# Rows of four weighted sums two fetches further behind their dots in TensorE's order

## The chip, the cores and the metric

The kernel runs on one core of a Trainium2 chip. The metric is the device time of one execution in microseconds (us): the median of several runs. Besides, one execution was profiled; its own time and its span are given apart, because all durations below come from that one execution. The engines are called by their short names: PE is TensorE (PEld its weight load), DVE is VectorE, ACT is ScalarE, POOL is GpSimd and SP is SyncE, which here only starts DMAs.

## What is computed

One layer of a streaming encoder over 576 tokens in two groups, A (192 tokens) and B (384 tokens). The token-mixing half (projection `w_in`, band attention, short convolution, gates, projection `w_o`) is followed by a retrieval half, and that one takes most of the time. For each token and each of 8 heads it picks the 16 best of 128 x 128 experts, and then gathers the chosen rows of two tables of 16384 x 1024 floats:

```python
idx = jnp.take_along_axis(cand_idx, pos, axis=-1)
g = jax.nn.softmax(top_s, axis=-1).astype(hb.dtype)
u = jnp.take(expert_u, idx, axis=0)
act = jax.nn.gelu(jnp.einsum("thkd,td->thk", u, hb))
vv = jnp.take(expert_v, idx, axis=0)
return jnp.einsum("thk,thkd->td", g * act, vv)
```

So each token has 128 dots with rows of `expert_u`, and its result is the sum of 128 rows of `expert_v` with the weights that come out of those dots.

## The kernel before, in words

**Tiles and fetches.** 32 tokens make a tile g (GT = 32; NG = 18 tiles). A tile has 32 fetches; fetch n = 32 g + j brings, for 128 pairs of a token and an expert, u and v side by side into one slot of the buffer `ring`: 128 x 2048 floats, 1 MB. Each fetch is an indirect DMA that POOL issues (L437), as soon as the fetch that last held the slot has been folded (semaphore `fold`). Up to fetch 192 (EARLY) the fetches have 8 slots, while 3 slots carry weight blocks that SP loads (L449); from there on they have all 11.

**The steps of a fetch.** DVE waits for the row and makes the dots (`dot`, L1492). ACT turns them into a small matrix of weights in three instructions (`spread`, L1081 to L1088, one place later: `gather(n)` on ACT spreads fetch n - 1). PE multiplies the v half by it into PSUM (`fold`, L825), always for four fetches in a row; the four go to four groups of 32 columns of the array. So a fold of four needs all four dots and spreads, and the four slots that it frees are those of the fetches eight further on: the fold of fetches 4K to 4K+3 lets POOL issue 4K+8 to 4K+11.

**After a tile** come `keep_sum` (ACT, L1095), `join` and `residual` (PE, L835 and L844), `scale` and `add` (DVE, L1501 and L1508) and `store`; for the next tile `natural` (PE, L805) and `keep_natural` (ACT, L1065) bring the tokens into rows, and for tiles 0, 4 and 6 `gate_rows` (PE, L813) the gate. They are hung on m, the fetch that is counted from behind n: `join` at j = 4 of the next tile, `residual` at 8, `natural` at 16, `keep_sum` at 31.

**What sets the order.** A list ORDER is written out by hand; each engine walks through it and does its own part of each entry. No engine reorders anything. Its stages, with the spans of the profiled execution:

- 320 to 470 us: retrieval of group A (`rt`; PE L745 and L725, DVE picks L1348 to L1395, `place` L794 on PE and L1478/L1481 on DVE, fetches 0 to 27 in groups of four, one group a head).
- 470 to 1045 us: the rest of group B's work, cut into ticks, stands between the fetches 28 to 171, about one tick a fetch: projection (`z`, L560 and L564), attention (`at`, scores L594, transposes L611, values L627), keys (`kn`, L660), merge (`mg`, L683 and L689), output projection (`wo`, L704), norm (L534) and retrieval (`rt`, L745 and L725).
- from 1075 us on: fetches alone.

PE's `join`, `residual`, `natural`, `gate_rows` and `place` share two PSUM banks. Each waits until the one before it in the order has been read (`g_free`). POOL issues fetches 4h to 4h + 3 of tile 0 only after DVE's `place(0, h)` (semaphore `placed_kept`).

In `merge`, DVE's first instruction for group B (L1317) writes over the buffer that the values leave from, so it waits for three stores `o_v_p` (L456). SP issues those when PE has finished the fourth merge tick and their turn in SP's list comes.

## Time and profile before

| what | value |
| --- | --- |
| median of 3 runs | 2088.72 us (2087.12 to 2089.95) |
| the profiled execution's own time | 2079.57 us |
| its span, first to last instruction | 2077.4 us |
| mean granted clock of TensorE | 0.957 |
| busy share of the span | PE 81%, DVE 59%, ACT 35%, POOL 29% |
| fetches | 576 of 1 MB, 71.3% of the 16 DMA engines' span |

A busy share is a mean over stages with different limits. The table of stretches shows the DMA engines full from about 1080 us to the end, and PE busy without a gap in much of what lies before. In a row of a timeline the brackets at the end give how long the engine had been idle before it and what released it. A matmul on f32 stands as two records; so one fold of four has 16.

### The profile page before, as it was taken

The numbers are of one execution on the slowest core, as the hardware profiler recorded it, in microseconds if no ns is written. First come the engines' busy times: TensorE is split into PE (matmuls) and PEld (weight loads), VectorE is DVE, ScalarE is ACT, GpSimd is POOL, SyncE is SP. The second block draws the span as 40 slices with busy tenths as digits, with TensorE's granted clock in tenths as the row PEclk, the third lists the DMA queues.
The fourth block names the chain that finished last, engine by engine and source line by source line (L and its number), as shares of the span: only waits on it lengthen the run. The fifth ranks groups of instructions, "written<-read, shape, count | busy, mean of one in ns | idle before, by whom it ended". The sixth has DMA issues, their size and how long they took to land.

```text
span 2077.4 us, 22509 instructions
## 1 busy us (share of the span) xinstructions
PE 1690.4 (81%) x7500; PEld 771.4 (37%) x7500; DVE 1221.6 (59%) x3212; ACT 724.9 (35%) x2231; POOL 607.4 (29%) x584
## 2 busy tenths in 40 slices
PE   6999997669978799989967777777777777777776
PEld 3864896435445455445522121121121121121111
DVE  3334116866565454447867777777677675555554
ACT  3125103442475223232343333333333343333332
POOL 0000001332322223222254434434444434333331
PEclk8999999779977999999999999999999999999999
DMA  9546514889965799967799999999999999999995
GB/s 400 212 173 255 221 52 167 341 336 385 358 235 199 315 400 370 421 254 276 269 373 422 421 421 422 421 421 421 421 421 421 422 421 422 421 422 421 421 421 240
DMA packets 102467, 718.50 MB, mean 346 GB/s; under 512 B 13584, under 2 KB 13584, under 8 KB 15696
## 3 DMA queue, kind: packets, MB, share of 16 engines
q0 software_dynamic: 82944, 604.02, 71.3%
q1 hardware_dynamic: 18544, 110.69, 13.6%
q10 hardware_dynamic: 864, 2.36, 0.3%
q8 instruction: 59, 0.97, 0.2%
q14 instruction: 56, 0.46, 0.1%
HBM read 712.30 MB, written 4.73 MB: 345 GB/s over the span
## 4 chain that ended last, share of the span: by engine, by line
DMA 41%; PE 30%; DVE 14%; issue 10%; ACT 4%; POOL 1%; SPq 0%; DVEq 0%; POOLq 0%; ACTq 0%
DMA ring<-in_expert_uv_dram,uidx 40%; PE ps L564 7%; PE ps L825 6%; PE ps L683 5%; DVE ring L1492 5%; PE ps L689 2%; PE ps L704 2%; POOL ring L437 1%; PE ps L560 1%; DMA ring<-in_wpack_dram 1%; PE ps L627 1%; PE ps L594 1%; PE ps L534 1%; ACT wdiag L1088 1%; DVE left L1393 1%
## 5 line engine op out<-in xcount | busy, mean ns | idle before, releaser
L825 PE MATMUL ps<-ring,wdiag 128*32 128x512 f32 x2304 | 866.6, 635 | 246.8 <-ACT wdiag L1088 228.0
L437 POOL DMA_INDIRECT ring<-in_expert_uv_dram,uidx x576 | 606.1, 1052 | 1387.0 <-PE ps L825 959.8
L1492 DVE CUSTOM_DVE_ANT_0 ring<-ring,mA 128x1024 f32<-128x1024 f32 x576 | 700.4, 1223 | 427.8 <-DMA ring<-in_expert_uv_dram,uidx 422.0
L825 PEld LDWEIGHTS ps<-ring,wdiag 128*32 128x32 f32 x2304 | 174.0, 114 | 881.0 <-ACT wdiag L1088 552.4
L1081 ACT ACTIVATE gel<-act_in 128x1 f32<-128x1 f32 x576 | 116.7, 203 | 875.5 <-DVE act_in L1492 875.0
L1088 ACT ACTIVATE wdiag<-repeat,wsel 128x32 f32<-128x32 f32 x576 | 185.1, 321 | 18.8
L1083 ACT ACTIVATE wsel<-gel,gsel 128x1 f32<-128x1 f32 x576 | 169.7, 295 | 18.7
L564 PE MATMUL ps<-hB,ring 128*128 128x384 f32 x320 | 109.3, 493 | 0.0
L745 PE MATMUL ps<-hB,ring 128*128 128x384 f32 x256 | 89.4, 504 | 8.5 <-issue 8.5
L683 PE MATMUL ps<-hB,ring 128*128 128x384 f32 x256 | 87.9, 498 | 9.8 <-DVE kv L1317 9.8
L564 PEld LDWEIGHTS ps<-hB,ring 128*128 128x128 f32 x320 | 59.0, 190 | 42.5 <-issue 6.3
L683 PEld LDWEIGHTS ps<-hB,ring 128*128 128x128 f32 x256 | 48.7, 194 | 48.3 <-DVE kv L1317 10.4
L745 PEld LDWEIGHTS ps<-hB,ring 128*128 128x128 f32 x256 | 49.2, 197 | 46.0 <-issue 17.7
L564 PE MATMUL ps<-hA,ring 128*128 128x192 f32 x320 | 56.7, 337 | 4.2 <-DVE qB L1212 4.0
L564 PEld LDWEIGHTS ps<-hA,ring 128*128 128x128 f32 x320 | 54.0, 197 | 7.3 <-issue 6.9
L745 PE MATMUL ps<-hA,ring 128*128 128x192 f32 x256 | 45.6, 338 | 6.7 <-DVE hA L1196 6.7
L1492 DVE DVE_READ_ACCUMULATOR2_ANT act_in<- 128x1 f32 x576 | 47.4, 82 | 0.0
L745 PEld LDWEIGHTS ps<-hA,ring 128*128 128x128 f32 x256 | 43.2, 197 | 8.1 <-ACT hA L909 6.9
L704 PE MATMUL ps<-kv,ring 128*128 128x384 f32 x128 | 42.9, 491 | 1.2 <-DVE kv L1325 1.2
L794 PE MATMUL ps<-chosen,ident 128*32 128x8 f32 (+1 forms) x368 | 8.2, 222 | 42.8 <-DVE chosen L1450 36.3
L683 PE MATMUL ps<-hA,ring 128*128 128x192 f32 x256 | 42.9, 326 | 0.0
L683 PEld LDWEIGHTS ps<-hA,ring 128*128 128x128 f32 x256 | 41.8, 190 | 0.0
(238 smaller groups left out, 1611.7 us busy)
## 6 DMA issues: line engine op xcount, KB each, us to landing
ring<-in_wpack_dram SPq DMA_DIRECT2D x96, 1024.0 KB, 8.9
ring<-in_expert_uv_dram,uidx POOLq DMA_INDIRECT x576, 22.7
xB<-in_x_b_dram SPq DMA_DIRECT2D x2, 1536.0 KB, 20.3
o_y_p<-mA ACTq DMA_DIRECT2D x16, 128.0 KB, 5.2
bias<-in_bias_dram SPq DMA_DIRECT2D x1, 1024.0 KB, 32.2
o_v_p<-kv SPq DMA_DIRECT2D x4, 256.0 KB, 11.1
o_k_p<-xB SPq DMA_DIRECT2D x4, 256.0 KB, 10.0
xB<-in_keysT_dram SPq DMA_DIRECT2D x1, 1024.0 KB, 9.6
```

Source lines behind the costliest of these rows:

```text
L437: nc.gpsimd.indirect_dma_start(out=ring[:, slot, :], out_offset=None, in_=ins["expert_uv"], in_offset=bass.IndirectOffsetOnAxis(ap=uidx[:, ...
L534: nc.tensor.matmul(ps[:, BK[g][0], 0:n], ones[:, :], tmp[g][:, t % 2, :], start=(t == 0), stop=(t == KD - 1)).then_inc(s[f"sq_used{g}"], 1)
L564: mm = nc.tensor.matmul(ps[:, bank, 0:n], w[:, t, c:c + P], h[g][:, t, :], start=(t == 0), stop=(t == KD - 1))
L683: mm = nc.tensor.matmul(ps[:, bank, 0:n], w[:, res, t, :], h[g][:, t, :], start=(t == 0), stop=(t == KD - 1))
L689: mm = nc.tensor.matmul(ps[:, bank, 0:n], w[:, d % 2, res - 2, t, :], src[:, t, :], start=(t == 0), stop=(t == 3))
L704: mm = nc.tensor.matmul(ps[:, BK[g][d % 2], 0:n], w[:, d % 2, t, :], mT[g][:, t, :], start=(t == 0), stop=(t == KD - 1))
L745: mm = nc.tensor.matmul(ps[:, BK[g][m], 0:n], w[:, m, t, :], h[g][:, t, :], start=(t == 0), stop=(t == KD - 1))
L825: mm = nc.tensor.matmul(pY[c * GT:(c + 1) * GT, half, :], wdiag[:, n % NDIAG, :], ring[:, ROW[n][0], D + half * 512:D + (half + 1) * 512], ...
L1081: nc.scalar.activation(gel[:, j:j + 1], act_in[:, g % 2, j:j + 1], ACT.Gelu_apprx_tanh).then_inc(s["gelu"], 1)
L1083: nc.scalar.activation(wsel[:, j:j + 1], gel[:, j:j + 1], ACT.Identity, scale=gsel[:, p % 2, a, j:j + 1]).then_inc(s["weight"], 1)
L1088: nc.scalar.activation(wdiag[:, n % NDIAG, :], repeat[:, :], ACT.Identity, scale=wsel[:, j:j + 1]).then_inc(s["diag"], 1)
L1492: nc.vector.tensor_tensor_reduce(r, r, h2n[:, g % 2, :], 1.0, 0.0, ALU.mult, ALU.add, act_in[:, g % 2, j:j + 1]).then_inc(s["dot"], 1)
```

## The change

A constant LATE = 3 takes the place of the number 1 in three places. Before, `gather(n)` with n = 4K + 5 folded fetches 4K to 4K+3 on PE; now this stands in `gather(4K + 7)`. m was n - 2 and is n - 4 on all engines, so the steps after a tile stand two fetches later on PE, ACT and DVE too. Dots, spreads, POOL's and SP's lists, `place` and the ticks stay where they are.

```diff
+LATE = 3
-    out += [("gather", NG * GT), ("gather", NG * GT + 1)]
+    out += [("gather", NG * GT + k) for k in range(LATE + 1)]
...
 def gather(n):   # PE
-    if n >= REP and n % REP == 1:
-        for k in range(n - 1 - REP, n - 1):
+    if n >= REP + LATE and n % REP == LATE:
+        for k in range(n - LATE - REP, n - LATE):
             fold(k)
-    m = n - 2
+    m = n - LATE - 1
     g, j = m // GT, m % GT
...
-    if n == NG * GT + 1:
+    if n == NG * GT + LATE:
...
 def gather(n):   # ACT, and DVE likewise
-    m = n - 2
+    m = n - LATE - 1
```

All lines of the changed kernel stand one further down. A row of the orders below is one instruction or several alike in a row: line, operation, output and inputs, size, count.

**Place 1, PE at the end of group A's retrieval.** L794 are the matmuls of `place`, L725 a head's key scores, L825 a fold of four, L805 `natural(1)`. Before:

```order
L794 MATMUL ps<-chosen,ident 32x2x4 x16
L825 MATMUL ps<-ring,wdiag 32x512 x8
L805 MATMUL ps<-ident,hA 32x128 x32
L725 MATMUL ps<-xB,kc 128x128 x2
L725 MATMUL ps<-xB,kc 64x128 x2
L794 MATMUL ps<-chosen,ident 32x2x4 x16
L825 MATMUL ps<-ring,wdiag 32x512 x8
L794 MATMUL ps<-chosen,ident 32x2x4 x16
```

The same place in the changed kernel:

```order
L795 MATMUL ps<-chosen,ident 32x2x4 x16
L826 MATMUL ps<-ring,wdiag 32x512 x8
L726 MATMUL ps<-xB,kc 128x128 x2
L726 MATMUL ps<-xB,kc 64x128 x2
L795 MATMUL ps<-chosen,ident 32x2x4 x16
L806 MATMUL ps<-ident,hA 32x128 x32
L826 MATMUL ps<-ring,wdiag 32x512 x8
L795 MATMUL ps<-chosen,ident 32x2x4 x16
```

`natural(1)` has moved past the key scores of the last head and past `place(0, 6)`, and stands ahead of the fold of fetches 16 to 19.

**Place 2, PE from the end of group B's attention into its merge.** L643 turns the last attention outputs, L660 are the key transposes, L683 the gate matmuls and L689 the two branch projections of the merge. Before:

```order
L643 MATMUL ps<-ident,xB 128x128 x4
L660 MATMUL ps<-ident,kv 128x128 x4
L825 MATMUL ps<-ring,wdiag 32x512 x8
L660 MATMUL ps<-ident,kv 128x128 x4
L805 MATMUL ps<-ident,hA 32x128 x32
L660 MATMUL ps<-ident,kv 128x128 x4
L683 MATMUL ps<-hB,ring 128x384 x8
L825 MATMUL ps<-ring,wdiag 32x512 x8
L683 MATMUL ps<-hB,ring 128x384 x8
L689 MATMUL ps<-qB,ring 128x384 x4
L689 MATMUL ps<-convB,ring 128x384 x4
L683 MATMUL ps<-hB,ring 128x384 x4
```

The same place in the changed kernel:

```order
L644 MATMUL ps<-ident,xB 128x128 x4
L826 MATMUL ps<-ring,wdiag 32x512 x8
L661 MATMUL ps<-ident,kv 128x128 x12
L826 MATMUL ps<-ring,wdiag 32x512 x8
L684 MATMUL ps<-hB,ring 128x384 x4
L806 MATMUL ps<-ident,hA 32x128 x32
L684 MATMUL ps<-hB,ring 128x384 x12
L826 MATMUL ps<-ring,wdiag 32x512 x8
L690 MATMUL ps<-qB,ring 128x384 x4
L690 MATMUL ps<-convB,ring 128x384 x4
L684 MATMUL ps<-hB,ring 128x384 x12
```

A fold that stood amid the four merge ticks has left them, and one stands now between the fourth tick and the first L690.

**Place 3, PE in group B's retrieval, last two heads.** L745 are the query matmuls (four a tick, four ticks a head), L725 the key scores. Before:

```order
L725 MATMUL ps<-bias,convB 128x128 x6
L745 MATMUL ps<-hB,ring 128x384 x8
L825 MATMUL ps<-ring,wdiag 32x512 x8
L745 MATMUL ps<-hB,ring 128x384 x4
L844 MATMUL ps<-ident,xA 32x128 x8
L745 MATMUL ps<-hB,ring 128x384 x4
L725 MATMUL ps<-bias,convB 128x128 x6
L825 MATMUL ps<-ring,wdiag 32x512 x16
```

The same place in the changed kernel:

```order
L726 MATMUL ps<-bias,convB 128x128 x6
L746 MATMUL ps<-hB,ring 128x384 x4
L836 MATMUL ps<-mA,repeat 32x512 x2
L746 MATMUL ps<-hB,ring 128x384 x12
L826 MATMUL ps<-ring,wdiag 32x512 x8
L726 MATMUL ps<-bias,convB 128x128 x6
L845 MATMUL ps<-ident,xA 32x128 x8
L826 MATMUL ps<-ring,wdiag 32x512 x16
```

A fold stands now right ahead of the last head's key scores, and `residual` (L845) behind them. From here on (fetch 172) the order of PE's own instructions is the same in both kernels but for that one.

## Rows read from the trace of the kernel before

**Rows 1.** Busy time of each engine, granted clock, DMA share, GB/s, in 40 us stretches
```profile
core 0: us, PE busy (x) PEld busy (x) DVE busy (x) ACT busy (x) POOL busy (x), PEclk, DMA share, GB/s
...
440.00:480.00 40.00, 32.42 (x163) 17.83 (x164) 21.18 (x55) 17.40 (x54) 17.52 (x16) 0.87 0.94 367
...
560.00:600.00 40.00, 30.66 (x152) 18.84 (x147) 25.00 (x66) 32.49 (x73) 9.75 (x9) 0.74 0.62 240
...
800.00:840.00 40.00, 40.00 (x200) 21.46 (x191) 17.21 (x34) 11.21 (x38) 11.39 (x10) 1.00 1.01 416
...
1200.00:1240.00 40.00, 31.59 (x144) 8.66 (x141) 29.09 (x77) 13.99 (x49) 16.42 (x17) 1.00 1.01 422
```

**Rows 2.** Fetches (L437) issued from 555 to 660 us
```profile
DMA to landing us min/median/max: 5.4/5.8/8.0
```

**Rows 3.** The same, issued from 820 to 842 us
```profile
DMA to landing us min/median/max: 9.8/13.3/13.4
```

**Rows 4.** The same, issued from 1200 to 1300 us
```profile
DMA to landing us min/median/max: 22.0/22.9/23.9
```

**Rows 5.** Timeline: start, duration, engine, line, operation [idle before, releaser], 423 to 447 us
```profile
423.99 3.52 PE L805 MATMUL ps<-ident,hA 128*32 128x128 f32 x64 [2.66 <-DVE gsel L1481]
...
440.27 1.67 POOL L437 DMA_INDIRECT ring<-in_expert_uv_dram,uidx  x1 [9.61 <-DVE gsel L1481]
...
446.76 0.61 PE L794 MATMUL ps<-chosen,ident 128*32 128x8 f32 x32 [9.15 <-DVE chosen L1450]
```

**Rows 6.** Timeline of PE, folds among the first ticks of group B
```profile
455.18 3.81 PE L825 MATMUL ps<-ring,wdiag 128*32 128x512 f32 x16
...
466.03 3.62 PE L825 MATMUL ps<-ring,wdiag 128*32 128x512 f32 x12
470.46 1.90 PE L825 MATMUL ps<-ring,wdiag 128*32 128x512 f32 x4 [0.81 <-ACT wdiag L1088]
```

**Rows 7.** Timeline, attention of group B: a fold, and an exponential's table load
```profile
558.37 2.89 PE L825 MATMUL ps<-ring,wdiag 128*32 128x512 f32 x12
...
561.99 1.91 PE L825 MATMUL ps<-ring,wdiag 128*32 128x512 f32 x4 [0.73 <-ACT wdiag L1088]
...
576.05 1.28 ACT L956 ACT_TABLE_LOAD   x1
```

**Rows 8.** Timeline, from the keys to the second merge round of group B
```profile
678.78 1.93 PE L825 MATMUL ps<-ring,wdiag 128*32 128x512 f32 x12
...
681.47 1.91 PE L825 MATMUL ps<-ring,wdiag 128*32 128x512 f32 x4 [0.76 <-ACT wdiag L1088]
...
688.57 2.74 PE L689 MATMUL ps<-qB,ring 128*128 128x384 f32 x8
...
703.05 0.56 DVE L1317 SCALAR_TENSOR_TENSOR kv<-tB,ps 128x384 f32<-128x384 f32 x1 [13.03 <-DMA o_v_p<-kv]
...
703.66 4.55 PE L683 MATMUL ps<-hB,ring 128*128 128x384 f32 x8 [9.77 <-DVE kv L1317]
```

**Rows 9.** Timeline, merge and output projection: PE, and a dot that waits
```profile
716.11 1.23 DVE L1492 CUSTOM_DVE_ANT_0 ring<-ring,mA 128x1024 f32<-128x1024 f32 x1 [5.29 <-DMA ring<-in_expert_uv_dram,uidx]
...
720.54 1.94 PE L825 MATMUL ps<-ring,wdiag 128*32 128x512 f32 x16
...
842.85 8.01 PE L704 MATMUL ps<-kv,ring 128*128 128x384 f32 x24 [1.24 <-DVE kv L1325]
```

**Rows 10.** Timeline of PE, retrieval of group B
```profile
912.59 11.04 PE L745 MATMUL ps<-hB,ring 128*128 128x384 f32 x24 [8.54 <-issue]
...
941.95 3.92 PE L825 MATMUL ps<-ring,wdiag 128*32 128x512 f32 x16
...
957.66 5.06 PE L825 MATMUL ps<-ring,wdiag 128*32 128x512 f32 x16
...
976.88 2.93 PE L725 MATMUL ps<-bias,convB 128*128 128x128 f32 x12 [2.31 <-ACT convB L1030]
...
1010.09 1.60 PE L725 MATMUL ps<-bias,convB 128*128 128x128 f32 x12 [0.57 <-ACT convB L1030]
```

More of the change, by code:

```diff
@@ L1119, in gather @@
                         store(g - 1)
-                    if n == NG * GT + 1:
+                    if n == NG * GT + LATE:
                         store(NG - 1)
@@ L1512, in gather @@
                         dot(n)
-                    m = n - 2
+                    m = n - LATE - 1
                     g, j = m // GT, m % GT
@@ L1528, in gather @@
                                 pass
-                    if n == NG * GT + 1:
+                    if n == NG * GT + LATE:
                         scale(NG - 1)
```

## Prediction

> **What bounds the kernel now.** I read the table of 40 us stretches first, then, stretch by stretch, which wait of each engine ends last, and last the timelines around the folds. From about 1080 us to the end the DMA engines are full at 422 GB/s [rows 1], so a fetch of 1.05 MB comes every 2.49 us, and it lands 22 to 24 us after it was issued [rows 4]: nine are queued, and no engine's order matters as long as that queue does not empty. So the time is fixed by when this stretch begins. It begins when group B's retrieval is over, that is, when PE has made the last head's key scores and DVE has picked from them. What is worth asking is how the change moves that moment (near 1045 us). Up to there 172 fetches and all of group B's ticks go through PE in a fixed order. PE has 40 busy us of 40 in most stretches [rows 1]; the exceptions are the attention (560 to 680 us), where PE, DVE and ACT go round in a ring and ACT has 32.49 of 40, and a few gaps named below. The chain of waits agrees: PE ticks, with a fold of 1.9 us between them.
>
> **What moves.** No work is added. Behind fetch 172 PE's order is the same, and POOL, with 11 slots, has 20 us of queue to hide two fetches; so I cost the last 1000 us at nothing. If that cover were gone, each 2.49 us of an idle DMA queue would count in full. Before it, each fold comes two fetches (two to three ticks) later. That has two sides. A fold waits less for its fourth dot. And the slots that it frees are asked for again later: fetch 4K+8 is wanted by DVE one fetch behind the fold instead of three.
>
> **1. Start of group B's projection.** `natural(1)` now stands behind `place(0, 6)` and so waits for DVE's copy of that, which is done at 439.8 us (POOL is released by it, 440.27) [rows 5]. It takes 3.52 us there, and the fold of fetches 16 to 19 is behind it; its first slot is free some 2 us into a fold. Fetches 24 to 27 then go out at 439.8 + 3.5 + 2 = 445.3 us, less about 1 us because the last head's scores no longer wait for `natural`: 4 us later than before, with the DMA engines nearly full (0.94) afterwards [rows 1]. Queued behind that wait are the fold, `place(0, 7)` and the first ticks. Against it, the two folds among the next ticks took 3.81 and 3.62 + 0.81 + 1.90 = 6.33 us, 10.1 in all [rows 6], where a fold without a wait takes 1.94 [rows 9]: 6.3 us of waiting that a later place can cover. But what they waited for was rows, and these now come 4 us later. Bounds -6.3 and +5; I take **-1**, nearer the middle because both hang on the same rows.
>
> **2. Attention of group B.** The fold at 558.37 ends at 563.90 [rows 7], 3.6 us longer than 1.94; two fetches later its spreads are long done: **-3.6**. For the six folds of this stage the other side counts. The DMA queue is near empty here (0.62), a fetch lands 5.4 to 8.0 us after issue, 5.8 in the middle [rows 2], and issue follows the fold by 0.3. DVE asks for it once it has dealt with one unit's scores, by my estimate 2 us behind the fold. So DVE waits about 6.1 - 2 = 4 us a fold, and ACT, which needs the dot before its next exponentials, behind it. Six times 4 is 24 us, the upper bound. The lower is nothing: ACT has its own backlog (a table load of 1.28 us [rows 7] twice for each pair of units), and the other three rows come 2.5 us apart while a unit takes 4, so the lag is made up before the next fold. I take 0.9 a fold, **+5.5**, near the lower end because ACT, not DVE, has the fuller row in this stretch.
>
> The Trainium skill puts a DMA from GpSimd at a fixed 2.0 us plus its bytes over 436 GB/s (DMA: Bandwidth & Descriptors, Anatomy of one DMA). That would be 4.4 us for a fetch, where the row has 5.8 at the median and never under 5.4; by the page DVE would wait 1.4 us less a fold and this term would be near nothing. The row decides.
>
> **3. Keys, and the wait for the stores.** PE stood idle 9.77 us from 693.9 us on, since L1317 waited for the stores of the values until 703.05, 14.5 us after the fourth merge tick (688.57) that let SP issue them [rows 8]. Ahead of them in the DMA queues were the four fetches of the fold that had ended at 683.4, up to 10 us of traffic. In the new order no fold stands amid the merge ticks (place 2): the last fetches were asked for 12 us before the fourth tick, so weights (1 MB) and stores (1.5 MB) meet an emptier queue, 2.5 MB at 0.42 plus about 2 to 3 us, so 8.5 us instead of 14.5. PE meanwhile has a fold and two ticks, 1.94 + 5.2 = 7.1 us, to do. From the fourth tick to PE's next merge round: 15.1 us before, about 8.9 now, -6.2. Having been idle, PE ran the first eight records in 4.55 us [rows 8] instead of some 2.6: -1.9. In return the three key transposes now stand behind a fold in one piece; the third waits for ACT's copy of the second, and that stands behind the spread of a fetch asked for by this very fold: 6.1 + 2.5 us. That is +3.7 against before, where the stage had waits of its own (0.76, and the fold of which that is the end took 4.6). Together **-4.4**; bounds -8 and 0.
>
> The skill says that each DMA engine takes turns between the queues it has work for, packet by packet (the same page, Queues, rings and completion order). By that, the fetches of the new fold, issued 2 us behind the fourth tick, share the engines with the stores instead of following them, and the term would shrink by some 2.5 us to -2. No row of before has this overlap; it speaks against the change and I leave it inside the bounds.
>
> **4. Merge and output projection.** PE is full here. With an unloaded queue the first row is there 5.3 to 6.1 us behind a fold (DVE waited 5.29 for it at 716.11 [rows 9]); DVE's merge steps behind such a dot are wanted by PE two ticks and a bit later, which is just enough: 0 to 1 us each, and I take 2 for the stage. From 800 to 880 us the DMA engines are full [rows 1] and landing takes 9.8 to 13.4 us [rows 3]; but that is backlog, and a fetch asked for 5 us later lands hardly later while there is one. At 842.85 PE waited 1.24 us for DVE's last merge [rows 9]; there both orders meet, and the new one has one fold of 1.94 more still to do. **+4**, bounds +1 and +8 (a dot that lands 4 us late at that point).
>
> **5. Retrieval of group B.** Two folds took 3.92 and 5.06 us [rows 10], since dots behind a pick were due: 2.0 + 3.1 = -5.1 gone. `residual` leaves the stretch behind the last scores: -1.9. One more fold falls into it, because the one that stood in the 8.54 us gap before 912.59 [rows 10] was free and is not now: +1.94. Two head changes lose the fold (one also `natural`) that covered ACT's copy of the queries, 0.57 to 2.31 us each [rows 10]: +2.6. Sum **-2.5**, bounds -6 and +1.
>
> **Sum.** -1 - 3.6 + 5.5 - 4.4 + 4 - 2.5 = -2.0 us. The profiled execution had 2079.57 us (span 2077.4, 2.2 around it), so 2077.6; the median of the runs is 9.15 us above it, and a difference carries over: 2088.72 - 2.0 = **2086.7 us**.
>
> **Rivals.** *The late rows cost nothing* (faster). Term 2 is then -3.6 alone and term 4 +1: -2.0 - 5.5 - 3 = -10.5, 2078 us. For it: ACT's fuller row, and the three later rows of each four come in time. Against it: in the ring of the attention nobody has 4 us to spare at each fold, PE least, at half clock (0.74 mean) [rows 1]. *The late first row is paid in full at each fold of the attention* (slower). DVE's wait of 4 us passes to ACT, ACT's to PE's transposes; at 2.7 us for each of six folds that is 16 instead of 5.5: +8.6, 2097 us. It decides from the point where ACT idles for a dot by over 1.5 us a fold there. For it: a fetch of 5.4 us at least [rows 2] against about 2 us of cover. *The start costs its full price*: term 1 at +5, so +4 in all, 2093 us. That the change does not do what it says I rule out: the orders show it.
>
> **How the numbers follow.** What a measurement of this kernel can tell from no change is about 0.2%, 4.2 us. Forecast (gains and late rows nearly cancel, -6 to +4): 0.42. Late rows free: 0.30. Paid in full: 0.20. The start at its full price: 0.08. Under 2084.5 us lie the second case and a part of the first, 0.35; above 2092.9 the third, half of the fourth and a little of the first, 0.27; between them 0.38. The range takes in the two outer cases' centres: 2077 to 2099.
>
> **What would show it.** Term 1: `natural(1)` ends near 443 and the fetch behind `placed_kept` comes 4 us later. Term 2: DVE waits for DMA between 560 and 660 us, where it had none, and ACT's waits for dots there are small. Term 3: L1317's wait for the stores is under 8 us and the kernel's worst PE gap is gone. Term 4: PE has gaps under 3 us in the merge. Term 5: no fold over 2.5 us in group B's retrieval. The forecast is wrong if the full DMA stretch begins over 4 us away from where it began, or if its 422 GB/s is not held.

## The result, and the profile after

The changed kernel is **slower by 1.0%**: 2110.47 us at the median (2104.75 to 2114.16) against 2088.39 us of the kernel before on the same chip; ratio 1.0103, 95% interval 1.0074 to 1.0132. That is 22 us more, where 2 us less was forecast, and outside the range of 2077 to 2099.

The profiled execution of after has 2114.16 us, its span is 2112.2 us and the mean granted clock 0.929 (0.957 before). Three lines of its page, from the head and from the costliest groups (busy us, mean ns of one | idle before it, and what ended most of that):
```profile
PE 1646.4 (78%) x7500; PEld 768.4 (36%) x7500; DVE 1223.7 (58%) x3212; ACT 726.2 (34%) x2231; POOL 619.4 (29%) x584
...
L1493 DVE CUSTOM_DVE_ANT_0 ring<-ring,mA 128x1024 f32<-128x1024 f32 x576 | 702.3, 1223 | 568.7 <-DMA ring<-in_expert_uv_dram,uidx 557.3
...
L826 PE MATMUL ps<-ring,wdiag 128*32 128x512 f32 x2304 | 790.6, 670 | 263.6 <-ACT wdiag L1089 179.2
```
PE is busy for 44 us less (1690.4 before), and yet the kernel takes longer: it is not PE's work that grew. The folds' records take 76 us less (866.6 before), PE's others 32 more. The mean clock says little here: most of its fall lies in the full DMA stretch (from 1100 to 2000 us it is 0.95 in after and 1.00 before, at 420 and 421 GB/s), and e2 below, which is faster than before, has 0.935. DVE's dots (line 1493 now) waited 557.3 us for rows, and 422.0 before.

To see where, I took from TensorE's timeline the start of the same instruction in each kernel and made stages of the differences. "Start" runs to the last `place` of the first four tiles, z to the first attention product of group B, attention and keys from there to its first merge product, merge to the first product of the output projection, that to the first retrieval product, retrieval to the last key scores; the last two are the pick behind it, up to `place(2)`, and the rest. "DVE" is what the dots waited for rows in attention and keys (us, times). All times in us, of the profiled executions; what e1 to e15 change is told below.

| kernel | start | z | att., keys | DVE | merge | out. proj. | retrieval | pick | rest | span |
| --- | --- | --- | --- | --- | --- | --- | --- | --- | --- | --- |
| before | 446.8 | 106.8 | 120.0 | 1.8, 1 | 169.3 | 69.7 | 130.7 | 24.8 | 1009.3 | 2077.4 |
| before, again (e5) | 448.1 | 108.1 | 125.0 | 5.7, 3 | 170.9 | 69.7 | 131.4 | 25.4 | 1009.2 | 2087.8 |
| **after** | 450.0 | 103.1 | 138.8 | 37.5, 15 | 178.9 | 72.8 | 130.3 | 27.8 | 1010.4 | 2112.2 |
| e1 folds only | 448.0 | 98.3 | 147.2 | 41.0, 17 | 172.4 | 71.8 | 133.8 | 24.4 | 1013.0 | 2108.8 |
| e2 rest only | 449.3 | 107.4 | 114.0 | 2.4, 1 | 172.9 | 68.1 | 129.9 | 26.6 | 1009.9 | 2078.2 |
| e3 six slots | 451.9 | 111.7 | 147.5 | 35.2, 12 | 185.7 | 72.3 | 140.4 | 25.8 | 1014.1 | 2149.3 |
| e4 all one later | 448.0 | 103.4 | 123.8 | 14.8, 12 | 170.9 | 69.7 | 123.6 | 25.4 | 1009.8 | 2074.6 |
| e6 folds in attention | 447.0 | 107.6 | 142.5 | 35.0, 13 | 170.9 | 69.7 | 131.4 | 25.4 | 1010.5 | 2105.0 |
| e8 mixed | 448.5 | 98.0 | 122.8 | 8.5, 6 | 171.1 | 68.1 | 124.0 | 26.6 | 1010.2 | 2069.4 |
| e13 attention's folds old | 448.6 | 101.3 | 115.6 | 7.1, 6 | 181.0 | 71.9 | 133.4 | 26.8 | 1010.3 | 2088.9 |

Against the two profiles of before, after loses 14 to 19 us in attention and keys, 8 to 10 in the merge, 3 in the output projection, 2 to 3 at the start and in the pick each and 1 in the rest, and wins 4 to 5 in z. The full DMA stretch at the end is as before; it begins later.

What a late row does is seen best in the attention of after. A fold, the fetch it lets go, the dot, an exponential, a transpose (start, duration, engine, line, operation [idle before, releaser]):
```profile
612.04 3.66 PE L826 MATMUL ps<-ring,wdiag 128*32 128x512 f32 x16
...
615.94 0.94 POOL L438 DMA_INDIRECT ring<-in_expert_uv_dram,uidx  x1 [18.03 <-PE ps L826]
...
622.04 1.23 DVE L1493 CUSTOM_DVE_ANT_0 ring<-ring,mA 128x1024 f32<-128x1024 f32 x1 [3.56 <-DMA ring<-in_expert_uv_dram,uidx]
...
624.60 0.61 ACT L957 ACTIVATE xB<-xB,stat 128x384 f32<-128x384 f32 x1 [3.75 <-DVE stat L1284]
...
625.81 0.87 PE L612 MATMUL ps<-ident,xB 128*128 128x128 f32 x3 [4.66 <-ACT xB L978]
```
The fold ends at 615.7 us and POOL, which had waited 18 us for it, issues at once. The row is there 6.1 us later. In that time DVE is done with one unit's scores and stands 3.56 us; the next unit's scores are behind that dot on DVE, ACT's exponential behind those, PE's transposes behind a copy of ACT. PE stands 4.66 us.

The sum for the stage, by DVE's dots alone (idle time by what ended it: us, times), first before, from 553 to 673 us:
```profile
L1492 DVE CUSTOM_DVE_ANT_0 ring<-ring,mA x27: 1214/1216/1280, 553.3 to 668.7; 128x1024 f32<-128x1024 f32 x27
...
  DMA ring<-in_expert_uv_dram,uidx: 1.8, 1
```
then after, from 553 to 691 us:
```profile
L1493 DVE CUSTOM_DVE_ANT_0 ring<-ring,mA x29: 1214/1224/1227, 552.9 to 690.5; 128x1024 f32<-128x1024 f32 x29
...
  DMA ring<-in_expert_uv_dram,uidx: 37.5, 15
...
  ACT gel L1082: 17.8, 7
```
One row in 27 was late before, 15 in 29 are now. The last line is who waited behind: ACT, 17.8 us over 7 times (7.1 over 2 before).

The keys, at the end of this stage, show the same in its longest form:
```profile
675.51 3.21 PE L826 MATMUL ps<-ring,wdiag 128*32 128x512 f32 x16
...
678.97 0.94 POOL L438 DMA_INDIRECT ring<-in_expert_uv_dram,uidx  x1 [15.70 <-PE ps L826]
...
684.51 1.23 DVE L1493 CUSTOM_DVE_ANT_0 ring<-ring,mA 128x1024 f32<-128x1024 f32 x1 [8.97 <-DMA ring<-in_expert_uv_dram,uidx]
...
685.78 0.20 ACT L1082 ACTIVATE gel<-act_in 128x1 f32<-128x1 f32 x1 [5.86 <-DVE act_in L1493]
...
687.19 1.12 PE L661 MATMUL ps<-ident,kv 128*128 128x128 f32 x4 [6.55 <-ACT xB L986]
```
Landing is 5.5 us here, and nothing covers it: DVE waits 8.97, ACT's spread 5.86, and PE 6.55 for a copy that stands behind the spread.

Next the wait for the stores, and further on the end of the merge. They answer to [rows 8] and [rows 9]:
```profile
708.17 2.85 PE L690 MATMUL ps<-qB,ring 128*128 128x384 f32 x8
...
718.22 0.56 DVE L1318 SCALAR_TENSOR_TENSOR kv<-tB,ps 128x384 f32<-128x384 f32 x1 [10.91 <-DMA o_v_p<-kv]
...
718.83 9.81 PE L684 MATMUL ps<-hB,ring 128*128 128x384 f32 x24 [5.23 <-DVE kv L1318]
...
846.60 10.77 PE L684 MATMUL ps<-hB,ring 128*128 128x384 f32 x24 [4.29 <-DVE kv L1318]
...
865.16 1.23 DVE L1493 CUSTOM_DVE_ANT_0 ring<-ring,mA 128x1024 f32<-128x1024 f32 x1 [9.16 <-DMA ring<-in_expert_uv_dram,uidx]
...
870.78 3.57 PE L705 MATMUL ps<-kv,ring 128*128 128x384 f32 x5 [3.60 <-DVE kv L1326]
```
The gap of 9.77 us is 5.23 now. From the end of the fourth tick (706.3 us, ahead of a fold of 1.94) to the next round it is 12.5 us instead of 15.1. But two new gaps, of 4.29 and 3.60 us, stand at the end of the merge, each behind a dot of DVE that waits for its row, and each time PE comes back slowly: 24 records take 10.77 us, where 24 of the same shape take 8.01 in a stretch without a gap [rows 9].

The granted clock shows the same in two stretches (columns as in [rows 1]):
```profile
560.00:600.00 40.00, 24.80 (x117) 15.28 (x117) 23.35 (x58) 27.56 (x64) 8.43 (x9) 0.63 0.61 238
...
840.00:880.00 40.00, 32.12 (x102) 16.09 (x101) 15.32 (x26) 8.83 (x32) 7.17 (x7) 0.83 0.70 283
```
In the first PE has 24.80 busy us and a mean clock of 0.63, against 30.66 and 0.74 [rows 1]. In the second the order of events can be read in steps of 2 us: the clock is 1.00 up to 844 us, while PE idles from 842.3 on, 0.50 (1.2 GHz) from 846 to 852, and 1.00 again behind 854. Here the idle time comes first, and the lower clock follows.

### The profile page after: what moved, and what is told of

Its sections match the earlier page's. It is cut to its first block, busy times and chain, and to the rows that moved or that the text cites. A ratio compares the mean times of both kernels' runs of the same rounds, so it can differ in the third digit from the quotient of the medians.

```text
span 2112.2 us, 22509 instructions
## 1 busy us (share of the span) xinstructions
PE 1646.4 (78%) x7500; PEld 768.4 (36%) x7500; DVE 1223.7 (58%) x3212; ACT 726.2 (34%) x2231; POOL 619.4 (29%) x584
## 4 chain that ended last, share of the span: by engine, by line
DMA 44%; PE 31%; DVE 10%; issue 9%; ACT 3%; POOL 3%; SPq 0%; DVEq 0%; POOLq 0%; ACTq 0%
DMA ring<-in_expert_uv_dram,uidx 43%; PE ps L565 7%; PE ps L826 7%; PE ps L684 4%; DVE ring L1493 3%; POOL ring L438 3%; PE ps L705 2%; PE ps L690 1%; PE ps L561 1%; DMA ring<-in_wpack_dram 1%; PE ps L746 1%; PE ps L595 1%; PE ps L628 1%; PE ps L845 1%; PE ps L535 1%
## 5 line engine op out<-in xcount | busy, mean ns | idle before, releaser
L1493 DVE CUSTOM_DVE_ANT_0 ring<-ring,mA 128x1024 f32<-128x1024 f32 x576 | 702.3, 1223 | 568.7 <-DMA ring<-in_expert_uv_dram,uidx 557.3
L438 POOL DMA_INDIRECT ring<-in_expert_uv_dram,uidx x576 | 618.1, 1073 | 1409.8 <-PE ps L826 970.9
L826 PE MATMUL ps<-ring,wdiag 128*32 128x512 f32 x2304 | 790.6, 670 | 263.6 <-ACT wdiag L1089 179.2
L826 PEld LDWEIGHTS ps<-ring,wdiag 128*32 128x32 f32 x2304 | 164.4, 118 | 828.1 <-ACT wdiag L1089 432.7
L684 PE MATMUL ps<-hB,ring 128*128 128x384 f32 x256 | 92.3, 517 | 10.4 <-DVE kv L1318 9.5
L746 PE MATMUL ps<-hB,ring 128*128 128x384 f32 x256 | 88.3, 499 | 10.4 <-DVE hB L1197 10.4
L565 PEld LDWEIGHTS ps<-hA,ring 128*128 128x128 f32 x320 | 54.0, 197 | 7.4 <-issue 7.0
L746 PEld LDWEIGHTS ps<-hA,ring 128*128 128x128 f32 x256 | 43.2, 197 | 8.5 <-ACT hA L910 6.9
L612 PE MATMUL ps<-ident,xB 128*128 128x128 f32 (+1 forms) x96 | 21.3, 325 | 26.4 <-ACT xB L978 17.9
```

Source lines behind the costliest of these rows:

```text
L438: nc.gpsimd.indirect_dma_start(out=ring[:, slot, :], out_offset=None, in_=ins["expert_uv"], in_offset=bass.IndirectOffsetOnAxis(ap=uidx[:, ...
L565: mm = nc.tensor.matmul(ps[:, bank, 0:n], w[:, t, c:c + P], h[g][:, t, :], start=(t == 0), stop=(t == KD - 1))
L612: mm = nc.tensor.transpose(ps[0:kw, bank, at:at + w], att_sc[0:w, u % 3, at:at + kw], ident[0:w, 0:w])
L684: mm = nc.tensor.matmul(ps[:, bank, 0:n], w[:, res, t, :], h[g][:, t, :], start=(t == 0), stop=(t == KD - 1))
L746: mm = nc.tensor.matmul(ps[:, BK[g][m], 0:n], w[:, m, t, :], h[g][:, t, :], start=(t == 0), stop=(t == KD - 1))
L826: mm = nc.tensor.matmul(pY[c * GT:(c + 1) * GT, half, :], wdiag[:, n % NDIAG, :], ring[:, ROW[n][0], D + half * 512:D + (half + 1) * 512], ...
```

## The experiments

Each run's time stands beside the kernel before on the same chip. Theory A: the folds free the slots later, so rows come late to DVE. Theory B: nothing is late, but what was moved now meets worse neighbours.

**e1, the folds alone.** From the changed kernel:
```
-                    m = n - LATE - 1
+                    m = n - 2                    # on PE, ACT and DVE
...
-                    if j == GT - 1 and g >= 0:
-                        keep_sum(g)
+                    if n > GT and n % GT == LATE:
+                        keep_sum(n // GT - 1)    # ACT
```


> Only the folds of four rows (and the copy of a tile's finished sum, which has to follow its last fold) stand at their new place, two fetches late; the natural rows, the joins, residuals, gate rows, scales, additions and stores stand where the kernel before has them. Theory A, late rows: a slot of the ring is freed two fetches later, so that the dot products on DVE find their rows missing; this has the whole loss, so the time is about 2110 us (2103 to 2116), the end of the second group's attention comes 7 to 10 us later than in the kernel before, and its last key scores about 30 us later. Theory B, moved work: what follows a tile (1024-column products on PE, copies of 1024 columns on ACT, two tensor products on DVE) now meets worse neighbours, and the loss comes from that; then this kernel is within 5 us of the kernel before.

Measured: 2118.73 us against 2087.43, ratio 1.0158 (1.0139 to 1.0177): **+31 us**. The folds hold more than the whole loss, and 2.7 us more than the upper end of what A expected. Attention and keys take 147.2 us. The last key scores come at 1071.5 us, 28 later than in the first profile of before.

**e2, the rest alone.** From the changed kernel:
```
-                    if n >= REP + LATE and n % REP == LATE:
-                        for k in range(n - LATE - REP, n - LATE):
+                    if n >= REP and n % REP == 1:
+                        for k in range(n - 1 - REP, n - 1):
```


> The folds stand where the kernel before has them; all that follows a tile (natural rows, gate rows, join, residual, the copies, scale, addition and store) stands two fetches later, as in the changed kernel. Theory A, late rows: no slot is freed later, so the time is that of the kernel before within 4 us (2085 to 2092 us). Theory B, moved work: the time is about 2105 to 2115 us.

Measured: 2076.86 us against 2087.43, ratio 0.9956 (0.9940 to 0.9971): **-10.6 us**. That is under what A expected (no change) and far from B. The two parts add up: +31.3 - 10.6 = +20.7, and the whole change has +22.1. Nearly all of the gain is in attention and keys, 114.0 us against 120.0 and 125.0; I did not look for which of the moved steps brings it.

**e3, late slots without a moved instruction.** In the kernel before, `row_slots`:
```
-        s = turn[n % NROW] if n < EARLY else turn[(n - EARLY) % NSLOT]
+        s = turn[n % 6] if n < EARLY else turn[(n - EARLY) % NSLOT]
```


> The kernel before, in which the rows of the first six tiles go round six slots of the ring instead of eight; not one instruction changes its place on any engine, and behind row 192 all eleven slots are used as before. Each fetch now starts just as far behind the dot of its row's time as in the changed kernel: row 4K+6 waits for the folds of quartet K at fetch 4K+5, where in the changed kernel row 4K+8 waits for those at fetch 4K+7. Theory A, late rows: the stages up to the last key scores lose what they lose in the changed kernel, 24 to 32 us there, and the whole is 2108 to 2120 us. Theory B, moved work: 2087 to 2092 us, since nothing is moved.

Measured: 2154.05 us, ratio 1.0329 (1.0310 to 1.0349): **+67 us**, in the direction of A and twice its size. In attention and keys it is what A says: 147.5 us (147.2 in e1), with DVE waiting 35.2 us for 12 rows. Elsewhere my equality of the two kernels fails: by the table, e3 is longer than e1 by 13 us each in z and in the merge and by 7 in retrieval. For the merge the trace shows why. There the early fold itself waits for the row that its own predecessor let go late. The folds of this stage in e3, from 711 to 897 us:
```profile
L825 PE MATMUL ps<-ring,wdiag 128*32 128x512 f32 x176 | 29.8, 608 | 7.0 <-ACT wdiag L1088 7.0
```
and in the kernel before, from 673 to 842 us:
```profile
L825 PE MATMUL ps<-ring,wdiag 128*32 128x512 f32 x176 | 23.4, 598 | 0.8 <-ACT wdiag L1088 0.8
```
Busy time and waiting together are 36.8 us against 24.2. A fold that stands later is itself spared this wait: in after, none of the 168 records between 691 and 870 us waited.

**e4, everything one fetch later instead of two:** `LATE = 2`.

> Folds and all that follows a tile stand one fetch later than in the kernel before instead of two. Theory A, late rows: a fetch is covered as long as the slot is freed more than one landing (5.8 us where the queue is empty) ahead of the dot; with one fetch less cover the loss is a third or less of the whole one where fetches take 5 to 8 us (attention +1 to +3 us), and near half where they take 10 to 13 us (keys and merge), so +6 to +11 us, 2095 to 2100 us. Theory B, moved work: no such rule; each product meets other neighbours than in either kernel, and any time between 2080 and 2115 us is possible.

Measured: 2076.71 us against 2087.43 (one of the five executions took 2106.57), ratio 0.9946 (0.9926 to 0.9965): **-10.7 us**, a gain where A expected a third to a half of the loss. Its stages say why. In attention and keys, DVE's waits grow from 1.8 or 5.7 to 14.8 us over 12 rows, but these are 1.2 us each, and the stage takes 123.8 us, inside what before itself shows. z takes 103.4 and retrieval 123.6, 3 to 5 and 7 to 8 us less. The first fetch of lateness is covered; the second is not.

**e5, the kernel before once more.**

> The kernel before, unchanged, for a second profiled execution of it. Against its first one (span 2077.4 us, second group's attention from 553.5, first merge product at 673.5, first product of the output projection at 842.9, last key scores at 1043.3) it shows how far the times of the stages move by themselves. Expected: each of these within 3 us, if two profiles can be compared stage by stage as the prediction did; if they move by 5 us or more, differences of that size between two profiles prove nothing.

Measured: span 2087.8 us, 10.4 more than in its first profile: 1.4 at the start, 1.3 in z, 5.0 in attention and keys, 1.6 in the merge, 0.7 or less in each later one. So single differences of 5 us in the attention prove nothing, and the 34.6 us between the two profiled executions that I first compared were 22 us of change, 9 us of a first one at the low end of its kernel and 4 us of a second one at the high end.

**e6, late folds beside the attention only.** From here on a general form of `gather` on PE is used, in which each quartet has its own lateness (1 is before, 3 is after), `rest_late` gives that of m, and `keep_late` that of `keep_sum`:
```
+def fold_late(k):
+    return 3 if 13 <= k <= 18 else 1
+def rest_late(n):
+    return 1
+def keep_late(n):
+    return 3 if 57 <= n < 80 else 1
...
+                    for late in range(LATE, -1, -1):
+                        q = (n - late) // REP - 1
+                        if (n - late) % REP == 0 and 0 <= q < NG * GT // REP and fold_late(q) == late:
+                            for k in range(REP * q, REP * q + REP):
+                                fold(k)
```


> The kernel before, with only the folds of the six quartets whose fetches run beside the second group's attention (rows 52 to 75) two fetches later, and the copy of the finished sum that has to follow the last of tile 1. Late rows: in the profile the stretch from the first attention product to the first merge product grows from 120 us to 140 to 147 us, DVE waits for rows of the gather there for 25 us or more in place of 1.8, and the whole is 2105 to 2115 us. Rival, the loss is spread over many stages in small parts: 2088 to 2098 us.

Measured: 2107.47 us against 2087.35, ratio 1.0102 (1.0085 to 1.0118): **+20 us from six folds**, 3.4 us each on average. Every other stage is as in e5 within 1.3 us. Up to the last unit's transposes (L643), with five of the folds, e6 takes 125.7 us against 112.3 and 114.3 in the two profiles of before; behind them, with the sixth fold right in front of the keys, 16.8 against 7.7 and 10.7. The dots from 554.5 to 697 us:
```profile
L1509 DVE CUSTOM_DVE_ANT_0 ring<-ring,mA x29: 1215/1217/1226, 554.3 to 696.1; 128x1024 f32<-128x1024 f32 x29
...
  DMA ring<-in_expert_uv_dram,uidx: 35.0, 13
...
  ACT gel L1096: 19.6, 6
```
ACT waited behind a late dot six times, 3.3 us each, where it had done so twice in before.

**e7, rest two later, folds one later:** `fold_late` 2, the other two 3.

> All that follows a tile stands two fetches later, as in the changed kernel, but the folds only one fetch later. If the two parts add up: the rest gives about -10 us, and the folds one fetch later give what the kernel with everything one fetch later shows beside the rest (about 0), so 2075 to 2080 us. If one fetch later is a gain of its own in the folds, it is 2066 to 2074 us.

Measured: 2078.09 us, ratio 0.9960 (0.9947 to 0.9974), as by the sum of the parts: the folds one fetch later cost or give nothing on top of the rest (e2).

**e8, mixed:** `fold_late` is 3 for k < 13, 2 for k >= 34 and 1 between; `rest_late` is 1 for n < 54 and 3 behind; `keep_late` is 3.

> Folds two fetches later while the second group's z runs (quartets 0 to 12), at their old place through attention, keys, merge and output projection (13 to 33), one fetch later from there on (retrieval and the fetches behind it); what follows a tile at its old place up to fetch 54, two fetches later from there. By the stages of the profiles so far: z -7 us (folds late, rest not), attention and keys -6 us (rest late), retrieval up to -7 us: about -10 to -20 us, 2068 to 2078 us. If the stage times of single profiles don't hold, it is no better than with the rest alone moved, 2077 to 2082 us.

Measured: 2068.42 us against 2087.35, ratio **0.9913** (0.9899 to 0.9927): faster than either kernel. z takes 98.0 us, retrieval 124.0.

**e9 to e11, half rows.** If the rows are the cause, the loss must go when the slots come back, with every instruction in its place. Half rows fit two to a slot, so ten places fit where eight whole rows were. These kernels leave out `expert_v`: the table that they gather from is `expert_u` alone, DVE's dots are as before, and a fold multiplies what the dot left in the slot in place of the v half. So they don't compute the layer; they serve to be compared with each other. The main lines of the edit:
```
+HALVES = 8                     # e9 (order of before), e10 (order of after); 10 in e11
...
+    turn = [2 * NRING + k for k in range(HALVES)]
...
-                        out=ring[:, slot, :], out_offset=None, in_=ins["expert_uv"],
+                        out=ring[:, slot // 2, slot % 2 * D:slot % 2 * D + D], out_offset=None, in_=ins["expert_uv"],
```


> The order of the kernel before, but each fetch brings only the first half of its row (4 KB for each partition in place of 8; the second half is left out of the computation, and the fold adds up the product of the first half instead). Eight places of half size for the rows. It is the base of the next two runs. Less traffic: faster than the kernel before in the fetches that stand alone at the end and wherever DVE waits for rows.

> The same half rows, eight places, in the order of the changed kernel. Late rows: the loss comes from the time in which a fetch lands after its slot was freed late; half the bytes land sooner (between half of 5.8 us and all of it), so the loss against the base e9 is clearly smaller than the 35 us (profile) that it is with whole rows: the stretch from the first attention product to the first merge product is 0 to 12 us longer than in e9 instead of 19. Rival, the loss sits in where the folds stand among TensorE's other products and not in the rows: the loss stays, 20 us or more against e9.

> As e10, with ten places for half rows in place of eight in the first six tiles: the two places give back the two fetches by which the folds are late. Not one instruction changes its place. Late rows: DVE waits for rows no more than in the base e9, and the stages up to the last key scores are as fast as in e9 or 5 to 15 us faster (the gain of what stands later behind a tile, and of the late folds in z and retrieval). Rival: as slow as e10, since the order is the same.

| | median us | z | att., keys | merge | retrieval | span |
| --- | --- | --- | --- | --- | --- | --- |
| e9, before's order, 8 places | 1749.73 | 100.1 | 121.5 | 164.6 | 128.9 | 1749.6 |
| e10, after's order, 8 places | 1752.30 | 98.1 | 126.2 | 160.1 | 125.7 | 1751.9 |
| e11, after's order, 10 places | 1740.22 | 98.4 | 112.9 | 159.7 | 125.5 | 1733.6 |

The ratios to the kernel before are 0.8421 (0.8403 to 0.8439), 0.8427 (0.8403 to 0.8450) and 0.8387 (0.8368 to 0.8406). DVE's dots in attention and keys, e10 from 541 to 667 us:
```profile
  DMA ring<-in_expert_uv_dram,uidx: 21.2, 9
...
  ACT gel L1083: 11.0, 5
```
and e11 from 542 to 655 us, where no line for the DMA is left:
```profile
L1494 DVE CUSTOM_DVE_ANT_0 ring<-ring,mA x28: 1214/1216/1224, 542.2 to 649.9; 128x1024 f32<-128x1024 f32 x28
...
its engine sat idle before it (us, times) until:
who waited for it (us, times):
  ACT gel L1083: 4.3, 1
```
With rows that land sooner, the loss against the same rows in the old order is 3 us (medians) and within the noise; two places more take 13.3 us off attention and keys, at the same order of instructions. This shows the late rows as the cause there. It does not for the merge and retrieval: the two places change 0.4 and 0.2 us in them, though DVE's waits for rows in the merge fall from 64.2 us to 11.7. With half rows these waits reach nobody; for whole rows in the merge the cause rests on e3, e13 and the traces. The three runs also show what the new order is worth without late rows: by the profiles e11 is 8.6 us faster than e9 in attention and keys, 4.9 in the merge and 3.4 in retrieval. The medians are 9.5 us apart, the spans 16.0; I take no finer number from it.

**e12, mixed, with the rest later already from fetch 24** (`rest_late` is 1 for n < 24, else as e8).

> As e8 (folds two fetches later up to quartet 12, at the old place up to 33, one later from 34), but what follows a tile stands at its old place only up to fetch 24, that is only the natural rows of tile 1, and two fetches later from there on. If the 5 us that z is faster with the rest at its old place (98 us in e8, 103 us in the changed kernel) come from the natural rows of tile 1 alone, this is as fast as e8 in z and up to 9 us faster in attention and keys (114 us where the rest alone was moved, 123 in e8): 2059 to 2068 us. If they come from the joins and copies of tile 0 behind fetch 33, it is 2068 to 2074 us.

Measured: 2068.62 us, but the kernel before had 2077.95 us beside it: ratio 0.9954 (0.9941 to 0.9967). The attention and keys took 121.5 us, not the 114 hoped for, and z 98.9. So the old place of the natural rows of tile 1 is enough for the z of e8, and the hoped 9 us aren't there.

**e13, the changed kernel with the folds of attention and keys at their old place** (`fold_late` is 1 for 13 <= k <= 20, else 3; the others 3).

> The changed kernel with the folds of quartets 13 to 20 (attention and keys of the second group) back at their old place; all else is as in the changed kernel. If the late rows of attention and keys are nearly the whole loss, that stretch takes 112 to 120 us in place of 138.8, and the whole is 2085 to 2091 us. If in addition the lateness is worth 6 us or more in the merge, as the one profile of the changed kernel says (178.9 us against 170.9), then the merge takes 176 us or more here too; if that was how merge and late attention meet, it takes 170 to 174 us, and the whole is 2078 to 2084 us.

Measured: 2092.14 us against 2078.46, ratio 1.0068 (1.0050 to 1.0086). Attention and keys take 115.6 us, 23 less than in after. The whole lies above the range that I gave, although the kernel before was 9 us faster here than where I had taken the range from: 13.7 us of loss stay, so attention and keys are not nearly all of it. The merge takes 181.0 us: the loss there stands by itself, it doesn't hang on a late attention. e8 and its repetition differ from e13 only by old folds in the merge and the output projection, folds one fetch later instead of two in retrieval and behind it, and `rest_late` before fetch 54. Against them e13 is 21.7 us slower by the median (2070.48 for the repetition on the same chip): 10 us in the merge, 4 in the output projection, 9 in retrieval, by the profiles.

**e14 and e15, e8 and e12 again, side by side.**

> e8 unchanged, on the same chip as e15. If the distance to the kernel before is a property of the program, the ratio is 0.990 to 0.993 again; if chips differ in it, it is nearer to the 0.995 that e12 showed where the kernel before took 2078 us.

> e12 unchanged, beside e14 on the same chip. Their profiles were alike in every stage (spans 2069.4 and 2068.6 us), so within 3 us of e14.

Measured: e14 2070.48 us, ratio 0.9959 (0.9945 to 0.9974); e15 2065.39 us, ratio 0.9941 (0.9927 to 0.9955); before 2078.46 us. The two are 5.1 us apart, where 3 were expected, but their intervals overlap. Both beat the kernel before; the changed kernel was not run beside them (2110.47 in its own runs). The distance to the kernel before is not a property of the program alone: before took 2087 to 2088 us beside after and e1 to e8 and 2078 beside e9 to e15, which ran on other chips and later, while the mixed kernels stayed between 2065 and 2071.

## Why the prediction was wrong

**What bounds the kernel:** right. The full DMA stretch was kept at its rate; its start moved, and the time with it.

**Term 1, start and z (-1):** right. `natural(1)` starts at 440.62 us after 7.10 us of waiting for DVE's copy and ends at 444.3; the next fetch goes out at 447.69 and `place(0, 7)` is 3.2 us later. z wins that back: seven folds take 17.5 us there, where there were eight with 23.5. At the first attention product after stands 0.5 us ahead of the first profile of before and 3 of the second.

**Term 2, attention (-3.6 and +5.5):** the first of two steps that failed (term 4 is the other). The mechanism was named; its price was not. The term's net is +1.9 us. e6, which has little but this mechanism and the keys, is 11 to 13 us longer up to the last unit's transposes, 2.3 to 2.7 a fold net of the -3.6, and 20 us in all. I took 0.9 a fold before the -3.6, for two reasons that the trace refutes. "The other three rows come 2.5 us apart while a unit takes 4, so the lag is made up": 15 rows waited, not one a fold, 2.5 us each, some of them hard behind one another (the keys above). "ACT, not DVE, has the fuller row": ACT had 32.49 us of 40, but its exponential stands behind DVE's scores, and these behind the dot, on one engine after the other; 7 idle us of 40 did not absorb 3.75 us at one point. The rival "paid in full" names this rightly (ACT idle for a dot by over 1.5 us a fold; 17.8 us over 7 times in after, 19.6 over 6 in e6), and its 2.7 us a fold is near what e6 has in the attention. In after this stage is only 7 to 9 us longer (121.4 against 112.3 and 114.3), because the rest, moved with the folds, gains there (107.5 in e2).

The Trainium skill's page that I weighed (DMA: Bandwidth & Descriptors, Anatomy of one DMA) gives an estimate of 4.4 us for a fetch and would have made the term near nothing. The fetches whose dots are shown above took 6.1 and 5.5 us, so the rule would have misled more than the row did.

**Term 3, keys and stores (-4.4):** right in direction for the stores, too small in both costs. From the end of the fourth tick to the next round it is 12.5 us, 2.6 less than before, where 6.2 less were forecast; L1317 (L1318 now) waited 10.91 us, not under 8, and the slow restart stayed (9.81 us for 24 records). SP issued the stores at 706.8 to 707.7 us and the last was in at 718.2, 11.9 us behind the tick where I had 8.5. The four fetches of the new fold went out from 708.48 on, in the same time; this fits the sharing that the prediction weighed at 2.5 us, but no run separates it. The keys cost more than the +3.7, which the rows given for it don't yield exactly (8.6 - 4.6 is 4.0): from the last unit's transposes to the first merge product it is 17.4 us in after, against 7.7 and 10.7, so +7 to +10. Of this 6.55 is the one wait shown, and 1.7 is a second fold (3.66) in place of `natural` (1.96).

**Term 4, merge and output projection (+4, bounds +1 and +8):** the second step that failed, and by as much as term 2. The two stages are 11 to 13 us longer although the stores' gap inside them gave 2.6 back, so the term is +14 to +15 in after. e13 and e8 set the folds' share at 14. "A fetch asked for 5 us later lands hardly later" holds while there is a backlog, and I took the backlog of before for granted. In after it runs out. The same 8 us of both, first after, then before (columns as in [rows 1], the last two the DMA share and GB/s):
```profile
852.00:860.00 8.00, 8.00 (x36) 3.92 (x35) 2.47 (x4) 1.90 (x7) 0.52 (x1) 0.99 0.02 7
...
852.00:860.00 8.00, 8.00 (x31) 4.42 (x24) 3.08 (x5) 2.43 (x7) 4.67 (x4) 1.00 1.01 421
```
The fetch that goes out next, at 859.48, is the one for which the dot at 865.16 waits 9.16 us: 5.7 us, as with an empty queue. DVE's waits for rows in the merge rose from 36.1 us (18 times) to 87.7 (37 times), and at the end of the merge PE waits behind them twice.

**Term 5, retrieval (-2.5):** right in sign and within its bounds, for after: -0.4 to -1.1. No fold is over 1.95 us, as forecast. But that is partly luck, the sum of a larger gain and a loss: one fetch later gives some 7 us (e4, e8), and the second gives it back, DVE waiting 27 us for rows there where it had not waited at all.

**The tail at nothing:** short by some 4 us, mostly before `place(2)`. **What I did not forecast at all** is the gain of the rest alone, -10.6 us (e2); its cause stays open. And my base: the one profile I measured against lay 10 us under a second one, half of it in attention and keys.

## What to carry to other kernels

How far a buffer's release may be moved back is set by one comparison: the time from release to landing (5.4 us at least here) against the time until the consumer, in its own order, asks; the first fetch of lateness was inside that cover and cost nothing (e7 against e2), the second cost 20 us for six folds (e6). Price a late row by the whole chain behind it (all that the waiting engine holds back for others), not by the idle share of the engines in that stretch, and count it for every row that can be late, not once a group. Where stages differ in what bounds them, set the release stage by stage: PE-bound z gained from late folds, the ring of the attention paid.

## What the runs showed of the hardware

Half the bytes shorten a fetch by little: 1 MB took 5.4 us at least [rows 2], 0.5 MB 4.3 us at least and 5.0 at the median in the same stage (e9, fetches from 543 to 664 us). So the half that was left out is worth about 1 us, and most of the landing time does not depend on the bytes. At the end, where whole rows keep the DMA engines full, the bytes count: the rest took 1009 us with whole rows and 697 with half ones. It is not halved, because another limit comes up: in e9, from 1100 to 1200 us, DVE is busy for 97.84 us of 100 and the DMA share is 0.87.

One and the same kernel before showed medians of 2087 to 2088 us in three sets of runs and 2078 in two, and two profiles 10.4 us apart, half of it in attention and keys, while the mixed kernels kept within 5 us. What sets this was not looked for.
